# Both feed-forward layers by Strassen's method, with the second layer's modulation on GpSimd

## The reference

```python
c_act = jax.nn.silu(c)
for i in range(2):
    mod = (c_act @ ada_w[i] + ada_b[i])[:, None, :]            # 1024 x 6144
    sh_m, sc_m, gt_m, sh_f, sc_f, gt_f = jnp.split(mod, 6, axis=-1)
    hn = rms_norm(h, norm_mix_w[i]) * (1.0 + sc_m) + sh_m
    y = even_mixer(hn, ...) if i % 2 == 0 else odd_mixer(hn, ...)
    h = h + gt_m * y
    hn = rms_norm(h, norm_ffn_w[i]) * (1.0 + sc_f) + sh_f
    gate, up = jnp.split(hn @ ffn_w_in[i], 2, axis=-1)         # 1024 x (2816 + 2816)
    h = h + gt_f * ((jax.nn.silu(gate) * up) @ ffn_w_out[i])   # 2816 x 1024
return rms_norm(h, final_norm_w)
```

## Time and profile before

| | |
|---|---|
| median of 3 runs | 1302.54 us (1300.65 to 1304.43) |
| profiled execution | 1305.82 us, span 1304.2 |
| PE busy | 1260.0 us, 97% |
| DVE busy | 864.0 us, 66% |
| ACT busy | 582.7 us, 45% |
| POOL busy | 181.0 us, 14% |
| mean granted clock of PE | 0.986 of full speed |

### The profile page before, as it was taken

One profiled execution on the slowest core, in us unless ns is written; L12 is line 12 of the kernel. 1 busy time (PEld: TensorE's weight loads), 2 busy tenths in 40 slices (PEclk: granted clock), 3 DMA queues, 4 the chain that ended last, 5 costly groups with the idle time before them and its releaser, 6 DMA issues.

```text
span 1304.2 us, 19810 instructions
## 1 busy us (share of the span) xinstructions
PE 1260.0 (97%) x7915; PEld 1073.5 (82%) x7915; DVE 864.0 (66%) x1045; ACT 582.7 (45%) x747; POOL 181.0 (14%) x242
## 2 busy tenths in 40 slices
PE   5999999899999999999999999999999999999997
PEld 3588788788788888888888888887879989988995
DVE  3799976567876663466467466455789458846865
ACT  6444752444432222222334476556575335523543
POOL 4007964930000000000000000000500000000000
PEclk8999999989999999999999999999999999999999
DMA  9593625425248763377233221112232243325212
GB/s 338 160 145 122 188 76 154 140 86 173 66 122 286 232 222 105 112 241 240 59 90 129 97 65 65 57 57 81 65 97 82 80 126 101 97 75 146 83 59 90
DMA packets 207475, 163.34 MB, mean 125 GB/s; under 512 B 31790, under 2 KB 197899, under 8 KB 205355
## 3 DMA queue, kind: packets, MB, share of 16 engines
q1 hardware_dynamic: 204496, 137.02, 36.3%
q0 software_dynamic: 2400, 25.20, 5.3%
q10 hardware_dynamic: 506, 0.12, 0.0%
HBM read 157.21 MB, written 4.19 MB: 124 GB/s over the span
## 4 chain that ended last, share of the span: by engine, by line
PE 76%; DVE 9%; POOL 5%; ACT 5%; issue 2%; DMA 1%; ACTq 0%; POOLq 0%; DVEq 0%; SPq 0%
PE banks L622 17%; PE banks L624 17%; PE banks L623 17%; PE banks L1365 5%; PE banks L1367 5%; PE banks L1366 5%; DVE wlo L2144 2%; PE banks L937 2%; PE banks L1272 1%; PE banks L927 1%; PE banks L1234 1%; DVE hn_lo L2194 1%; POOL scan_a L3048 1%; DMA raw<-in_ffn_w_in_dram 1%; DVE tmp L2188 1%
## 5 line engine op out<-in xcount | busy, mean ns | idle before, releaser
L2144 DVE TENSOR_TENSOR wlo<-raw,whi 128x2048 fp32r<-128x2048 f32 (+4 forms) x116 | 229.1, 1976 | 87.5 <-ACT whi L1529 41.4
L622 PE MATMUL banks<-hn_hi,whi 128*128 128x512 f32 x688 | 273.8, 398 | 5.2 <-DVE hn_lo L2292 2.2
L624 PE MATMUL banks<-hn_hi,wlo 128*128 128x512 f32 x688 | 270.2, 393 | 0.0
L623 PE MATMUL banks<-hn_lo,whi 128*128 128x512 f32 x688 | 270.2, 393 | 0.0
L622 PE MATMUL banks<-ff_hi,whi 128*128 128x512 f32 x416 | 163.3, 392 | 0.0
L624 PE MATMUL banks<-ff_hi,wlo 128*128 128x512 f32 x416 | 162.0, 389 | 0.0
L623 PE MATMUL banks<-ff_lo,whi 128*128 128x512 f32 x416 | 162.0, 389 | 0.0
L622 PEld LDWEIGHTS banks<-hn_hi,whi 128*128 128x128 f32 x688 | 130.5, 190 | 36.0 <-DVE hn_lo L2194 3.5
L624 PEld LDWEIGHTS banks<-hn_hi,wlo 128*128 128x128 f32 x688 | 130.4, 190 | 27.7
L623 PEld LDWEIGHTS banks<-hn_lo,whi 128*128 128x128 f32 x688 | 130.7, 190 | 26.2
L1535 ACT ACTIVATE whi<-raw 128x2048 fp32r<-128x2048 f32 (+1 forms) x35 | 65.3, 1866 | 148.8 <-PE banks L624 148.8
(11 more groups left out here) (569 smaller groups left out, 2647.0 us busy)
## 6 DMA issues: line engine op xcount, KB each, us to landing
raw<-in_ffn_w_in_dram SPq DMA_DIRECT2D x88, 512.0 KB, 4.9
ada_in<-in_ada_w_dram POOLq DMA_DIRECT2D x16, 1536.0 KB, 6.3
raw<-in_sb_w_in_dram SPq DMA_DIRECT2D x24, 512.0 KB, 4.4
raw<-in_hy_w_in_dram SPq DMA_DIRECT2D x20, 512.0 KB, 5.9
ada_in<-in_ada_w_dram SPq DMA_DIRECT2D x18, 512.0 KB, 4.4
ada_first<-in_ada_w_dram SPq DMA_DIRECT2D x8, 1024.0 KB, 15.0
raw<-in_ffn_w_out_dram SPq DMA_DIRECT2D x32, 256.0 KB, 3.1
raw<-in_ffn_w_out_dram SPq DMA_DIRECT2D x16, 384.0 KB, 4.0
```

The costliest lines, as they stand in the source:

```text
L622: pe.matmul(o, lh, rh, start=first, stop=False)
L623: pe.matmul(o, lh, rl, start=False, stop=False)
L624: return pe.matmul(o, ll, rh, start=False, stop=last)
L2144: TTO(wlo[s][:, 0:width], raw[s][:, 0:width], whi[s][:, 0:width].bitcast(F32), SUB)\
```

## The change

1. **The first FFN gets the second's form.** Both are now built by one function `ffn(L)` per engine, with `THIRDS = ((6, 8, 8), (8, 8, 6))`: 4 plain slots, 18 Strassen slots, and three output stages in place of two, of 6, 8 and 8 tiles a block. A fourth of the normalised input's low half now holds a fourth operand, and some PSUM banks and semaphores change hands (`seven` becomes `six`).
2. **The second layer's modulation goes to POOL.** 48 tiles of 128x1024, six parts of eight. For each tile POOL issues the load (L2991 of the changed kernel) into one of two buffers, multiplies it in place (L3009) and adds it to the accumulator (L3011); the first of a part is multiplied straight into it (L3007). It starts at the first Strassen slot. At each part's start it waits for DVE's fold of the part before, and at the fifth part's start for the end of the first FFN. Folds stand on DVE in the first FFN after a slot (parts 0 and 2), in an output stage (parts 1 and 3), and in the attention stage after the first head of a pair (parts 4 and 5).
3. **Layer 0's gate tiles** go into the out-projection: four ahead of the first residual, one each after residuals 0, 1, 2 and 4.
4. **SP** queues the loads of `y_s` ahead of all scale tiles; before, three scale tiles stood ahead of them.

```diff
-HALVES = (12, 10)
-FT = sum(HALVES)
+FT = 22
 PLAIN = 4
-THIRDS = (8, 8, 6)
+THIRDS = ((6, 8, 8), (8, 8, 6))
...
-            sp.wait_ge(ada_used, 18)
-            for t in range(2, 5):
-                scale_tile(t)
             sp.wait_ge(y_out, 128)
             for t in range(4):
                 sp.dma_start(y_s5[:, t, :, :],
                              y_dram[:, t * P:(t + 1) * P, :].rearrange("i p c -> p i c")).then_inc(y_in, 16)
-            for t in range(5, 8):
+            sp.wait_ge(ada_used, 18)
+            for t in range(2, 8):
                 scale_tile(t)
...
+            def ada1_fold(part):
+
+                dve.wait_ge(ada_used, 32 + 8 * (part + 1))
+                if part == 3:
+                    dve.wait_ge(mod_sum, 5)
+                fold((ada1_acc, ada2_acc)[part // 4], (0, 1, 0, 0, 1, 2)[part]).then_inc(c_ready, 1)
...
                     residual(unit + m + 1, banks_of[m], gate, m)
+                    if m in (0, 1, 2, 4):
+                        gate_tile(4 + (0, 1, 2, 2, 3)[m])
...
-                            if ada_i is not None:
-                                dve.wait_ge(ada1_ld[s], 64 * half + 16 * ada_i)
-                                dve.wait_ge(ada_used, 30 + 8 * half + s + 2 * ada_i)
-                                STT(ada1_acc[:, :], ada1_in[s][:, :], c_act[:, bass.ds(ada_i * 2 + (s - 2), 1)],
-                                    ada1_acc[:, :], MUL, ADD).then_inc(ada_used, 1)
...
+            FOLD_IN_SLOT = {(0, 1, 1): 0, (0, 2, 3): 2}
+            FOLD_IN_STAGE = {(0, 1, 0): 1, (0, 2, 4): 3}
...
+                        if not last:
+                            low_sums(q + 1)
+                        if (L, t, q - qs[0]) in FOLD_IN_SLOT:
+                            ada1_fold(FOLD_IN_SLOT[(L, t, q - qs[0])])
...
                 if p_ < 2:
+                    ada1_fold(4 + p_)
                     next_lo(p_ + 1, 2)
...
-            pool.wait_ge(ada_used, 32)
-            for half in range(2):
-                with pool.Fori(1, 5) as i:
-                    for s in range(2):
-
-                        pool.wait_ge(ada_used, 29 + 8 * half + s + 2 * i)
-                        pool.wait_ge(block_done, B_FF0 + 2)
-                        src = ada_w[1].rearrange("(p t) n -> p (t n)", t=8)[
-                            :, bass.ds(i * (2 * 6 * D) + (s - 2) * 6 * D + half * 3 * D, 3 * D)]
-                        pool.dma_start(ada1_in[s][:, :], src).then_inc(ada1_ld[s], 16)
+            def ada1_load(u):
+
+                part, t = u // 8, u % 8
+                if u == 32:
+                    pool.wait_ge(block_done, B_SB)
+                pool.dma_start((ada1_in if u < 32 else ada2_in)[u % 2][:, :],
+                               ada_w[1].rearrange("(p t) n -> p t n", t=8)[:, t, part * D:(part + 1) * D])\
+                    .then_inc(ada1_ld[u % 2], 16)
+
+            pool.wait_ge(t_summed, after_one(4))
+            ada1_load(0)
+            ada1_load(1)
+            for u in range(48):
+                part, t = u // 8, u % 8
+                in_, acc = (ada1_in[u % 2], ada1_acc) if u < 32 else (ada2_in[u % 2], ada2_acc)
+                pool.wait_ge(ada1_ld[u % 2], 16 * (u // 2 + 1))
+                if t == 0:
+                    if u > 0:
+                        pool.wait_ge(c_ready, 3 + part)
+                    else:
+                        pool.wait_ge(t_done, after_ada(4))
+                    pool.tensor_scalar(acc[:, :], in_[:, :], c_act[:, t:t + 1], None, MUL).then_inc(ada_used, 1)
+                else:
+                    step(pool.tensor_scalar(in_[:, :], in_[:, :], c_act[:, t:t + 1], None, MUL))
+                    pool.wait_ge(ada_used, 32 + u)
+                    pool.tensor_tensor(acc[:, :], acc[:, :], in_[:, :], ADD).then_inc(ada_used, 1)
+                if u == 31:
+                    ada1_load(32)
+                    ada1_load(33)
+                elif u < 46 and u != 30:
+                    pool.wait_ge(ada_used, 33 + u)
+                    ada1_load(u + 2)
```

More of the change, by code:

```diff
@@ L588, in hidden_slot, with middle_slot @@
+            def middle_slot(L, n, tile):
                 b = n % 2
@@ L1192, in _, with plain_slot @@
-            ffn(0, 16, B_FF0, 1)
+            def plain_slot(L, j, between=None):
+                n = IN_SLOT[L][0] + j
+                slot_ready(n)
+                mh, ml = halves(whi[n % 2]), halves(wlo[n % 2])
+                for two in range(2):
+                    if j == 2:
+                        pe.wait_ge(pair_steps, pair_value(2 * L + 1, 1))
+                    else:
+                        pe.wait_ge(block_free, 2 * n + two - 3)
+                    for k in range(KT):
+                        last = pass3(bank[2 * (j % 2) + two][:, :], mh[:, k, two, :], ml[:, k, two, :],
+                                     hn_hi[:, k, :], hn_lo[:, k, :], k == 0, k == KT - 1)
+                        if between is not None and two == 1 and k == 5:
+                            between()
+                    last.then_inc(block_done, 1)
@@ new lines, in out_block @@
+            def out_block(L, t, m, between=None):
+                n, n_in = OUT_SLOT[L][t] + m, THIRDS[L][t]
+                mh, ml = (x_[n % 2][:, 0:n_in * P].rearrange("p (k m) -> p k m", k=n_in) for x_ in (whi, wlo))
+                slot_ready(n)
+                pe.wait_ge(block_free, 2 * n - 6 if m >= 4 else 2 * OUT_SLOT[L][t] - 2)
+                for k in range(n_in):
+                    if m == 0 and k == n_in - 1:
+                        pe.wait_ge(block_free, 2 * OUT_SLOT[L][t])
+                    last = pass3(bank[m % 4][:, :], mh[:, k, :], ml[:, k, :], ff1_hi[:, k, :], ff1_lo[:, k, :],
+                                 k == 0, k == n_in - 1)
+                    if between is not None and k == 1:
+                        between()
+                last.then_inc(block_done, 2)
@@ L1418, in _ @@
[L1418 to L1429 removed]
+            ffn(1)
@@ L2036, in _ @@
+            late_norm(3, 72, S_FF1, B_FF1)
+            ffn(1)
             norm_root(4)
@@ new lines, in sums_of, with first, second, third @@
+            def sums_of(q):
+                b = Q_SLOT[q] % 2
+                a11, a12, a21, a22 = (raw[b][:, 512 * n:512 * n + 512] for n in range(4))
+                s3, s2, s4 = (sum_full[q % 2][:, n, :] for n in range(3))
+                def first():
+                    dve.wait_ge(raw_in[b], 32 * (Q_SLOT[q] // 2 + 1))
+                    if q >= 2:
+                        dve.wait_ge(six, after_one(6 * (q - 2) + 6))
+                    TTO(s3, a11, a21, ADD).then_inc(w_sums, 1)
+                def second():
+                    dve.wait_ge(w_sums, after_one(4 * q + 1))
+                    TTO(a21, a21, a22, ADD).then_inc(w_sums, 1)
+                    TTO(s2, s3, a22, ADD).then_inc(w_sums, 1)
+                def third():
+                    dve.wait_ge(w_sums, after_one(4 * q + 3))
+                    TTO(s4, s2, a12, ADD).then_inc(w_sums, 1)
+                return first, second, third
```

1030 lines of the change are left out of this document (427 added, 603 removed).

## The result

The changed kernel takes 1358.41 us (median of 4 runs, 1356.89 to 1359.05) against 1301.6 us for the kernel before in the same comparison: a ratio of 1.0433, with a 95% interval from 1.0400 to 1.0466. The forecast was 1315.7, its range 1295 to 1334. The sign was right, but the loss is 57 us where 13 were forecast.

A forecast was written before the change was run, and what follows sets the result against it. PE, busy 97% of the span, was taken as the bound, with DVE's spare time at risk. -14.4 - 1.5 + 14 + 7.6 + 2.5 + 1.5 + 3.5 = +13.2 on 1302.54 gave about 1315.7 us, range 1295 to 1334.

The forecast's parts named there:

- Gain on PE: First FFN: 18 plain slots of 10.88 us become Strassen slots of 10.08, winning 14.4 us.
- Gain in the S5 stage: S5 stage: scale tiles on POOL start later and no longer hold up ys_lo, winning 1.5 us.
- What POOL's work costs in a Strassen slot: First FFN: POOL additions block DVE, multiplies do not; 1.0 us in each of 14 slots, 14 us (2.8 to 33).
- The first third's end: First FFN: PE stalls 4.6 us behind short blocks, plus POOL's additions 1.5 and half clock 1.5: 7.6 us (4.6 to 10.4).
- The second third's end: First FFN: a stall of about 1.0 us plus 1.5 for POOL's work beside it: 2.5 us.
- The last output stage: First FFN: with shorter blocks PE runs into a late residual some 1.4 us earlier, costing 1.5 us (0 to 3).
- The waits for folds: First FFN: POOL waits 15 to 20 us for DVE's folds, which costs nothing.
- rival 4: First FFN: DVE waits for POOL at a fold, late folds delay PE: 1335 to 1340 us; chance 0.06.
- The attention stage: POOL's parts 4 and 5: one addition delays DVE's chain in each of two pairs, costing 3.5 us (0 to 7).
- The signs: Profile after: slots 11 to 12 us beside additions, wlo 3 to 4.6, PE idle 4 to 7; wrong if multiplies lengthen operations.
- The rivals: DVE absorbs it, 1297 (0.25); it cancels, within 4 us (0.12); multiplies block too, 1355 (0.05); late folds, 1335 to 1340 (0.06).
- Rival 3: Slots beside POOL: a multiply holds DVE for its whole 2.84 us, 40 us more, 1355 us; chance 0.05.

The follow-up runs named there:

- experiment 1: Changed kernel with POOL's modulation arithmetic left out, loads, waits and folds kept (loads only): 1303.8 us, ratio 1.0003 to the kernel before.
- experiments 10 and 11: Changed kernel with the modulation on DVE instead of POOL, thirds 8, 8, 6, in two placements of tiles: 1307.4 and 1308.5 us, ratios 1.0025 and 1.0055.

## Why the prediction was wrong

The sum was +13, the result +57. The step that failed is the price of POOL's arithmetic on DVE, in two of its terms: the attention stage (3.5 forecast, 23 measured) and the Strassen slots (14 forecast, 23 measured). Of the 44 us between the two sums these are 29, the ends of the thirds some 5, the gain in the S5 stage 1.5; the rest, about 9, no row here assigns.

**Gain on PE**, -14.4: right as a count, and the slots without POOL beside them take the 10.1 us. It did not reach the time even without POOL's arithmetic: 12 of it went into PE's waits and half clock at the places that experiment 1 shows.

**Gain in the S5 stage**, -1.5: not seen, and smaller than the noise.

**What POOL's work costs in a Strassen slot**, 1.0 us (0.2 to 2.4) in each of 14: the price failed. A full slot took 14.25 instead of 10.08, 4.2 more. The count failed the other way, and hid part of it: POOL waited 31 to 34 us at each of the four folds, not 15 to 20, so in the last two thirds its work lay beside seven slots, not twelve. Against the loads-only kernel the second third lost 14.4 us and the last 9.0. That is 23.4, inside the term's bounds of 2.8 to 33 only because two errors met. Three numbers in the price were wrong, all on the same side:
- An addition was taken at 1.7 us, 2.35 less the 28% of a slot in which DVE has no operation with two SBUF inputs. It cost 2.2. The share holds for a DVE that has time to spare; in the full slots each addition found a two-input operation waiting.
- A multiply was taken at nothing. In a full slot it cost 0.5 to 0.9. The row I rested this on, `y_s` at 252.59, began 1.28 us after the multiply, behind the part that keeps DVE out. The rival that priced the whole 2.84 was wrong too.
- The slot that gets longer takes in more of POOL: 2 tiles, not 1.4. Then 2 x 2.2 + 0.9 + 0.5 = 5.8, less the spare 1.48, is 4.3; measured 4.2. The bounds missed it because even the upper one kept 1.4 tiles and the free multiply.

The forecast weighed a rule against itself. The Trainium skill's "SBUF — State Buffer", section "SBUF: two separate sides", says that whichever of the two starts first gets the pair of ports for the whole instruction, and the other blocks. The runs agree with that for additions (2.2 of their 2.4 us) but not for multiplies: about 1.0 of 2.85 us is held, and by the recorded starts the multiply at 476.38 held a sum that had begun at 476.33.

**The first third's end**, 7.6: the short blocks' 4.6 measured 4.67 with loads only; with POOL it was 6.51, and 2.12 more for a late `ff_lo` ahead of the stage (406.13). With about 1.5 for the clock that makes 10.1, near the forecast's upper end.

**The second third's end**, 2.5 (1 to 5): 5.36. POOL's arithmetic did this too. Four of DVE's operations in the chain that PE waited for are together 4.0 us longer beside it; the first of them, the addition beside it, and PE's wait:

```profile
576.52 2.48 DVE L2568 TENSOR_TENSOR sum_full<-raw 128x512 f32<-128x512 f32 x1 [0.73 <-DMA raw<-in_ffn_w_in_dram]
```

```profile
576.06 2.40 POOL L3011 TENSOR_TENSOR ada_acc<-ada_acc,ada_in 128x1024 f32<-128x1024 f32 x1
```

```profile
589.60 0.58 PE L1127 MATMUL banks<-hn_hi,whi 128*128 128x256 f32 x1 [5.36 <-DVE wlo L2068]
```

The loads, which the forecast left out, are a smaller part: the weights took 6.1 us to land instead of 5.3. Before, POOL's loads came one to a slot; now it loads the next tile as soon as a buffer is free.

**The last output stage**, 1.5: 0.3. **The waits for folds**: POOL waited at four of them and DVE for POOL at none, so rival 4 never came near.

**The attention stage**, 3.5 (0 to 7): 23 more than in the kernel before, 26 more than in the same kernel without parts 4 and 5. This is the largest miss, and far outside its bounds. The step looked at one chain and counted one addition in it for each pair; it overlooked the norm ahead of the stage (9 us of waits) and the rest of the 14 additions. The stage is not short of DVE's time, since 16 fused tiles on DVE cost it nothing where DVE waits (experiments 10 and 11). But POOL's additions fall where POOL's own pace puts them, and there they hold `hn_lo`, `wlo` and `later_lo`, for which PE waits.

**The signs.** PE's idle of 4 to 7 us ahead of the second third, with half clock behind it, came (6.51). The slots of 11 to 12 us did not (12.7 to 14.3), and a sign of being wrong did: operations long beside multiplies.

**The rivals**: none of them. Rival 3's 1355 is near 1358 by luck: its mechanism, a multiply that holds DVE for its whole length, is refuted by the run with multiplies only (1310). DVE became the engine that sets the pace, and the list did not have that as a case of its own.
